# Rotation tables turned once and copied by six DMAs; GpSimd's product of growth and C in four pieces

## The reference, cut to what matters

```python
def rope(x, positions):
    half = HEAD_DIM // 2                      # 32
    inv = 1.0 / (ROPE_THETA ** (jnp.arange(half) * (2.0 / HEAD_DIM)))
    ang = positions[..., None] * inv
    cos, sin = jnp.cos(ang)[:, :, None, :], jnp.sin(ang)[:, :, None, :]
    x1, x2 = x[..., :half], x[..., half:]
    return jnp.concatenate([x1 * cos - x2 * sin, x2 * cos + x1 * sin], axis=-1)

# in ssd_mixer: what the state carried into a chunk adds to its outputs
    y_off = jnp.einsum('bclgn,cbgjpn->bclgjp', cm, prev)
    y_off = y_off * jnp.transpose(jnp.exp(a_cs), (0, 3, 4, 1, 2))[..., None]
```

## Time and profile before

| what | value |
|---|---|
| median of 3 runs | 1017.61 us (1017.61 to 1017.72) |
| the profiled execution | 1017.64 us |
| its span | 1015.9 us |
| busy: TensorE, VectorE, ScalarE, GpSimd | 1007.2, 638.2, 481.0, 115.9 us |
| TensorE clock granted | 2.4 GHz level, mean 0.998 of full speed |

### The profile page before, as it was taken

The page is one execution under the profiler, slowest core; times in us unless marked ns, Lnnn a source line. Parts: engine busy times, 40 slices in busy tenths (PEclk is TensorE's granted clock), DMA queues, the critical chain, the costliest instruction groups (busy, mean ns, idle before and its releaser), DMA issues.

```text
span 1015.9 us, 13424 instructions
## 1 busy us (share of the span) xinstructions
PE 1007.2 (99%) x5127; PEld 835.9 (82%) x5127; DVE 638.2 (63%) x853; ACT 481.0 (47%) x825; POOL 115.9 (11%) x172
## 2 busy tenths in 40 slices
PE   9999999999999999999999999999999999999997
PEld 8888788878878887888888888998888888888886
DVE  6798898889879888542322333776666666632114
ACT  6668757755865778232211232644344344331121
POOL 6023003300410320000000030200000000000001
PEclk9999999999999999999999999999999999999999
DMA  6433541435344232423233426233243343232312
GB/s 205 142 119 131 167 118 54 155 125 145 95 166 125 94 130 79 135 83 124 83 110 97 165 83 190 60 84 83 83 121 85 83 122 84 83 125 85 123 42 83
DMA packets 119226, 113.36 MB, mean 112 GB/s; under 512 B 13999, under 2 KB 108811, under 8 KB 119179
## 3 DMA queue, kind: packets, MB, share of 16 engines
q1 hardware_dynamic: 119179, 112.72, 35.5%
HBM read 109.94 MB, written 2.77 MB: 111 GB/s over the span
## 4 chain that ended last, share of the span: by engine, by line
PE 89%; DVE 4%; ACT 3%; POOL 1%; DMA 1%; issue 1%; SPq 1%; DVEq 0%; POOLq 0%; ACTq 0%
PE ps L1476 21%; PE ps L1478 20%; PE ps L1477 20%; PE ps L1485 5%; PE ps L1483 5%; PE ps L1484 5%; PE ps L1604 3%; PE ps L1675 2%; PE ps L1676 2%; PE ps L1677 2%; PE ps L1800 2%; DVE conv L1105 1%; PE ps L1811 1%; DVE wlo L974 1%; PE ps L1640 1%
## 5 line engine op out<-in xcount | busy, mean ns | idle before, releaser
L974 DVE TENSOR_TENSOR wlo<-raw,whi 128x2048 fp32r<-128x2048 f32 (+2 forms) x82 | 184.0, 2245 | 200.4 <-ACT whi L535 200.0
L1476 PE MATMUL ps<-uhi,whi 128*128 128x512 f32 x768 | 301.3, 392 | 0.0
L1478 PE MATMUL ps<-uhi,wlo 128*128 128x512 f32 x768 | 299.0, 389 | 0.0
L1477 PE MATMUL ps<-ulo,whi 128*128 128x512 f32 x768 | 298.9, 389 | 0.0
L535 ACT ACTIVATE whi<-raw 128x2048 fp32r<-128x2048 f32 (+2 forms) x82 | 153.8, 1877 | 167.1 <-PE ps L1485 93.0
L1478 PEld LDWEIGHTS ps<-uhi,wlo 128*128 128x128 f32 x768 | 144.2, 188 | 30.3
L1476 PEld LDWEIGHTS ps<-uhi,whi 128*128 128x128 f32 x768 | 144.2, 188 | 30.1 <-issue 0.8
L1477 PEld LDWEIGHTS ps<-ulo,whi 128*128 128x128 f32 x768 | 144.3, 188 | 29.1
L1405 DVE SCALAR_TENSOR_TENSOR yT<-ps,fpar,yT 128x511 f32<-128x511 f32 x88 | 65.7, 749 | 36.6 <-ACT yT L931 35.0
L931 ACT ACTIVATE yT<-ps,fpar 128x512 f32<-128x512 f32 x44 | 34.1, 780 | 97.8 <-DVE fpar L1400 68.0
L1476 PE MATMUL ps<-rhi,whi 128*128 128x512 f32 x192 | 74.8, 390 | 0.0
(11 more groups left out here) (270 smaller groups left out, 1432.5 us busy)
## 6 DMA issues: line engine op xcount, KB each, us to landing
raw<-in_w_in_dram SPq DMA_DIRECT2D x24, 1024.0 KB
raw<-in_w_up_dram SPq DMA_DIRECT2D x44, 512.0 KB
raw<-in_w_down_dram SPq DMA_DIRECT2D x11, 1024.0 KB
sums_bc<-sum_rows_scratch SPq DMA_DIRECT2D x16, 512.0 KB, 3.9
raw<-in_w_ssd_out_dram SPq DMA_DIRECT2D x8, 1024.0 KB
raw<-in_w_in_dram SPq DMA_DIRECT2D x15, 512.0 KB
grow_bc<-sum_rows_scratch SPq DMA_DIRECT2D x12, 512.0 KB, 5.8
raw<-in_w_attn_out_dram SPq DMA_DIRECT2D x4, 1024.0 KB
```

The lines of the kernel that those rows point to most:

```text
L974: dve.tensor_tensor(wlo[sl][:, 0:width] if into is None else into, raw[sl][:, 0:width], h.bitcast(F32), ALU.subtract).then_inc(s["lo_done" ...
L1476: pe.matmul(bank(b)[:, span], hi_[:, k, c], ah[:, span], start=first and k == ks[0], stop=False)
L1477: pe.matmul(bank(b)[:, span], hi_[:, k, c], al[:, span], start=False, stop=False)
L1478: ins = pe.matmul(bank(b)[:, span], lo_[:, k, c], ah[:, span], start=False, stop=last and k == ks[-1])
```

## The change

The tables are no longer repeated before they are turned: VectorE writes cos (32 columns) and sin (64 columns) side by side, TensorE turns 96 rows in four transposes, ScalarE copies one bank, and six DMAs write the repetitions into the scratch. The product on GpSimd is issued as four instructions of two heads (256 columns) each, and the counts of `grown` become four times as large for all who wait for it.

```diff
@@ SP
             def spread_growth(g, t):
-                sp.wait_ge(s["grown"], g * (NT - 1) + t - 1)
+                sp.wait_ge(s["grown"], 4 * (g * (NT - 1) + t - 1))
...
                 if g == 0:
-                    sp.wait_ge(s["tab_sb"], 2)
-                    sp.dma_start(tab_scr, x_tok[:, 0:2, :]).then_inc(s["tab_out"], 16)
-                    sp.wait_ge(s["tab_out"], 16)
+                    sp.wait_ge(s["tab_sb"], 1)
+                    for b in range(4):
+                        sp.dma_start(tab_scr[HALF * b:HALF * (b + 1), 0, :], x_tok[0:HALF, 0, :]).then_inc(s["tab_out"], 16)
+                    for b in range(2):
+                        sp.dma_start(tab_scr[HD * b:HD * (b + 1), 1, :], x_tok[HALF:HALF + HD, 0, :]).then_inc(s["tab_out"], 16)
+                    sp.wait_ge(s["tab_out"], 16 * 6)
@@ GpSimd
-                        pool.wait_ge(s["tab_mm"], 2)
+                        pool.wait_ge(s["tab_mm"], 1)
...
-                    pool.tensor_tensor(c_dec[:, :, :], grow_bc[:, :, :],
-                                       conv[:, 5, (t + 1) * P:(t + 2) * P].unsqueeze(1).to_broadcast([P, SH, P]),
-                                       ALU.mult).then_inc(s["grown"], 1)
+                    for q in range(4):
+                        pool.tensor_tensor(c_dec[:, 2 * q:2 * q + 2, :], grow_bc[:, 2 * q:2 * q + 2, :],
+                                           conv[:, 5, (t + 1) * P:(t + 2) * P].unsqueeze(1).to_broadcast([P, 2, P]),
+                                           ALU.mult).then_inc(s["grown"], 1)
@@ ScalarE
-                    for w in range(2):
-                        act.wait_ge(s["tab_mm"], w + 1)
-                        act.activation(x_tok[:, w, :], bank(6 + w), ACT.Copy).then_inc(s["tab_sb"], 1)
+                    act.wait_ge(s["tab_mm"], 1)
+                    act.activation(x_tok[0:HALF + HD, 0, :], ps[0:HALF + HD, 6, :], ACT.Copy).then_inc(s["tab_sb"], 1)
...
-                act.wait_ge(s["grown"], G * (NT - 1))
+                act.wait_ge(s["grown"], 4 * G * (NT - 1))
@@ VectorE
-            dve.tensor_copy(c_dec[:, 0:4, :].rearrange("p t (b k) -> p t b k", b=4),
-                            cosT[:, :, :].unsqueeze(2).to_broadcast([P, NT, 4, HALF])).then_inc(s["tab_rep"], 1)
-            dve.tensor_copy(c_dec[:, 4:8, :].rearrange("p t (b k) -> p t b k", b=2),
-                            sinT[:, :, :, :].rearrange("p t r k -> p t (r k)").unsqueeze(2).to_broadcast([P, NT, 2, HD])).then_inc(s["tab_rep"], 1)
+            dve.tensor_copy(c_dec[:, 0:4, 0:HALF], cosT[:, :, :]).then_inc(s["tab_rep"], 1)
+            dve.tensor_copy(c_dec[:, 0:4, HALF:HALF + HD], sinT[:, :, :, :].rearrange("p t r k -> p t (r k)")).then_inc(s["tab_rep"], 1)
@@ TensorE
-                pe.wait_ge(s["grown"], G * (NT - 1) + t)
+                pe.wait_ge(s["grown"], 4 * (G * (NT - 1) + t))
...
-                    for w in range(2):
-                        for t in range(NT):
-                            ins = pe.transpose(ps[:, 6 + w, t * P:(t + 1) * P], c_dec[:, 4 * w + t, :], ident[:, :])
-                        ins.then_inc(s["tab_mm"], 1)
+                    for t in range(NT):
+                        ins = pe.transpose(ps[0:HALF + HD, 6, t * P:(t + 1) * P], c_dec[:, t, 0:HALF + HD], ident[:, :])
+                    ins.then_inc(s["tab_mm"], 1)
...
-                            pe.wait_ge(s["tab_sb"], 2)
```

More of the change, by code:

```diff
@@ L473, in group @@
                 pool.wait_ge(s["blocks_ok"], 4 * (G + 1))
-                pool.wait_ge(s["tab_out"], 16)
+                pool.wait_ge(s["tab_out"], 16 * 6)
                 for i, j in POOL_MOVES:
@@ L622, in move_x @@
                     act.wait_ge(s["blocks_ok"], 4 * (G + 1))
-                    act.wait_ge(s["tab_out"], 16)
+                    act.wait_ge(s["tab_out"], 16 * 6)
                     to, of = block_move(i, j)
```

## The result

The changed kernel takes 1019.53 us (median of 22 runs, 1019.23 to 1020.29) against 1017.74 (median of 22 runs, 1017.23 to 1018.55): the ratio is 1.0018, 95% interval 1.0012 to 1.0025. It is slower by 1.8 us, inside what I had called within 0.2%. Forecast were +5.0 us.

The account below looks back on a forecast made before the run. TensorE, issuing almost without pause, was taken as the bound. Stalls of 2.3, 2.2 and 0.9 us in steps 1 to 3, less 0.4 for transposes, gave +5.0: 1017.64 to 1022.6 us, range 1018.2 to 1025.0.

Parts of the forecast that it names:

- The bound: Whole kernel: TensorE issues almost without pause, busy 1007.2 of 1015.9 us; time is gained only by giving it less.
- Part 1: Rotation tables: four transposes fewer on TensorE give -0.4 us; the six DMAs cost 0.
- E: Extra length of GpSimd's product of growth and C in four pieces: 3 x (0.18 + 0.06) = 0.72 us.
- Step 1: Step t = 1, four times: L1227 0.65 us later, TensorE has 0.06 us to spare, stalls about 0.57 us.
- Step 2: Step t = 2, four times: L1225 to L1227 each blocked, 0.70 us later, 0.14 to spare; stall 0.56 us.
- Step 3: Step t = 3, three times: the third product reaches TensorE late, stall about 0.3 us.
- its signs: TensorE's waits would list L485 and L1233 with about 0.5 us, four times each, and the product three times.
- The pieces cost little: Rival, chance 0.16: smaller or no fixed part per piece on GpSimd, giving 1020.1 down to 1017.7 us.
- estimate from the Trainium skill: GpSimd's product: 0.06 us fixed per instruction, estimated from 4497 ns for 2048 columns, giving about 1018.9 us.
- VectorE slips in early: Rival, chance 0.14: small softmax operations pass between pieces, no stall in steps t = 1 and 2; 1017.2 us.
- The exclusion of VectorE and GpSimd: VectorE instructions with two SBUF inputs and GpSimd instructions reading SBUF exclude each other for a whole instruction.

Follow-up runs that it names:

- part 1 alone: Only the smaller rotation tables (four transposes, six DMAs), product whole again, against the kernel before: 1017.23 against 1017.76 us, ratio 0.9994.
- the added product: Old tables, whole product, plus a 128-column product into an unneeded tile ahead of it, against the kernel before: 1022.03 against 1017.62 us, 1.0045.

## Why the prediction was wrong, point by point

- **The bound** was right: TensorE issues without pause, and all of the 1.8 us are gained or lost on it.
- **Part 1** was right: -0.4 forecast, 0.43 us of transposes by the trace, 0.5 by medians. The DMAs cost nothing, with the next load 0.6 to 1.3 us later. Their issue was mis-sized: with part 1 alone the six took from 35.17 to 38.78, 3.6 us and not 2.5.
- **E was mis-sized: the term that carried the forecast.** The length of a piece was right (0.735 forecast, 0.739 measured). The gap was not: I took 0.06 us from copies of 32 partitions, and it is -0.04. The nearest row stood in the earlier trace rows: L497 ended at 98.11 and L485, the same kind of operation, had started at 98.06. E is 0.42 us instead of 0.72. With 0.30 us less in each stall, the prediction's own sum would be 4 x 0.27 + 4 x 0.26 + 0 - 0.4 = 1.7 us, near the measured 1.8. That nearness is luck: it has 1.0 us in step 2, where nothing came, and nothing in step 3, where 1.3 us came.
- **Step 1, the room.** L1228 is late by 0.43, forecast were 0.65. "Some 0.06 us" to spare was wrong: TensorE's load had come 0.22 us ahead of its matmul (91.22 and 91.44), and in the changed kernel load and matmul both start at 91.69. The room is 0.28 us; on the other hand the second matmul loses 0.11 (1.13 us for the pair instead of 1.02). The stall is 0.25, forecast 0.57.
- **Step 2: the mechanism came, the size did not.** All three operations were blocked as described, but L1228 ends together with GpSimd's L488, while before it ended 0.22 us behind it. So it is 0.21 late and not 0.70, and the load's head start is room here too (0.31 us before, 0.13 in the changed kernel). No stall where I had 2.2 us. The delay reappears in step 3.
- **Step 3: the wrong waiter.** I looked at the product (0.3 us). The product comes only 0.06 to 0.11 us late; what waits is the diagonal product, for the masked decay (L1215), which stands behind the small operations on VectorE and had nothing to spare: 0.42 us together. The prediction followed the small operations to xdt and to the probabilities and left out this third user of the same queue. Of its signs, TensorE's list shows neither L1233 nor the product, and for L485 only the weight load waits (0.41 us).
- With these terms the sum is 4 x 0.25 + 0 + 3 x 0.42 - 0.4 = 1.9 us, measured 1.8.
- **The rivals.** "The pieces cost little" named the outcome, at E between 0.18 and 0.48, though its reason, a smaller fixed part, did not hold; nor did it for the estimate from the Trainium skill (GPSIMD Engine Reference, Elementwise — side-by-side cycle accounting), 1018.9, which came nearer than mine: the fixed part is 0.18 us by the pieces as by the row, 0.06 by the estimate from the page, and it is the overlap that brings a further piece down to 0.14 us. "VectorE slips in early" did not happen with four pieces, and with eight it happened in part, at a price of 1 us of occupation.
- The exclusion of VectorE and GpSimd, which the Trainium skill states (SBUF — State Buffer, Who interferes with whom), held in every trace: L1226 took 0.48 to 0.58 us in the changed kernel and 1.18 with the added product instead of 0.16, and L485 took 1.44 when it was second. The prediction's wording, two inputs in SBUF, is too narrow for these rows: the negation, with one, took 0.97 us before and 0.67 in the changed kernel instead of 0.17.

## What to carry to other kernels

Where two engines exclude each other, the length of an instruction on one is also the wait of the other, and more instructions are a longer occupation: weigh the further piece (here 0.14 us) against the wait that it cuts, and ask first whether that wait costs anything at all; before the change it cost TensorE nothing. When a chain of operations is delayed, list everything behind it in the queue with its own room, not only what the chain is for. For the cost of one more instruction, take the row in which the same operation follows itself or its like, and for the room at TensorE count the head start of its weight load.

The tables' part alone was the better kernel: 1017.23 us, against 1017.76 before in the same series and 1019.53 with both parts in the first, though its gain over the kernel before is within the interval.

## What the runs showed of the hardware that I had not expected

- Products on GpSimd that follow each other overlap by 0.04 us, while its copies lie 0.06 us apart.
- A matmul that waits for its own weights starts with their load (both at 91.69 us), and it is its successor that takes 0.11 us longer.
- The same instruction L485 started 0.17 or 0.48 us after its last input, depending on 16 instructions that had long been done; as the engine that comes first holds up the other, those 0.3 us became a stall of 0.64.
